# A hybrid decoder trunk with grouped experts: row numbers cast earlier, the first expert load by table held behind a row gather

## The reference

```python
scores = sigmoid(hf @ w_router)                      # 512 x 16 experts
group  = argmax(sum of the top 2 biased scores of each of 4 groups)
expert = the 2 best experts of that group            # 1024 assignments
gate   = their scores, normalised to sum 1
# tokens are sorted by expert into blocks; each block runs one expert:
yb  = (silu(xblk @ w_gate[e]) * (xblk @ w_up[e])) @ w_down[e]
out = zeros.at[buf_tok].add(yb * buf_w)              # back to the tokens
```

## Time and profile before

| | us |
|---|---|
| median of 3 runs | 1586.93 |
| lowest and highest | 1586.53 and 1590.78 |
| the profiled execution | 1591.75 |
| its span | 1590.0 |
| PE busy (88% of the span) | 1401.6 |
| DVE busy (41%) | 644.2 |
| ACT busy (20%) | 313.4 |
| POOL busy (5%) | 77.0 |

### The profile page before, as it was taken

One profiled execution on the slowest core, in us unless ns is written; L12 is line 12 of the kernel. 1 busy time (PEld: TensorE's weight loads), 2 busy tenths in 40 slices (PEclk: granted clock), 3 DMA queues, 4 the chain that ended last, 5 costly groups with the idle time before them and its releaser, 6 DMA issues.

```text
span 1590.0 us, 22845 instructions
## 1 busy us (share of the span) xinstructions
PE 1401.6 (88%) x9981; PEld 730.1 (46%) x9981; DVE 644.2 (41%) x1001; ACT 313.4 (20%) x525; POOL 77.0 (5%) x231
## 2 busy tenths in 40 slices
PE   5999999967888788889999958998998879999992
PEld 2445566536767633633333334555654353333331
DVE  1114334235756523723332334565742372233234
ACT  2221211133333202100000023442121310000002
POOL 7100000000000000000000020000000000000002
PEclk9999999987988989999999979999999898999997
DMA  9695676002000102899999962111100389999994
GB/s 359 218 316 185 212 243 205 3 29 92 3 2 3 56 0 119 338 392 425 350 426 421 398 217 88 54 54 53 53 1 1 136 349 391 427 347 426 422 382 172
DMA packets 87696, 332.63 MB, mean 209 GB/s; under 512 B 6456, under 2 KB 37420, under 8 KB 70188
## 3 DMA queue, kind: packets, MB, share of 16 engines
q1 hardware_dynamic: 74336, 290.04, 47.0%
q10 hardware_dynamic: 7788, 21.19, 3.4%
q0 software_dynamic: 5472, 19.93, 3.3%
HBM read 308.60 MB, written 22.54 MB: 208 GB/s over the span
## 4 chain that ended last, share of the span: by engine, by line
PE 70%; DVE 14%; DMA 9%; ACT 4%; issue 2%; POOL 0%; SPq 0%; DVEq 0%; ACTq 0%; POOLq 0%
PE banks L1352 16%; PE banks L1809 15%; PE banks L1830 9%; PE banks L1725 5%; DVE work L1945 5%; PE banks L1393 4%; PE banks L1341 4%; DMA h_features<-in_w_up_dram 3%; PE banks L1268 2%; DMA h_features<-in_w_down_dram 2%; PE banks L1709 2%; DVE work L1951 2%; DMA work<-h_rows,idx_tok 1%; PE banks L1518 1%; DMA ring<-in_w_ada_dram 1%
## 5 line engine op out<-in xcount | busy, mean ns | idle before, releaser
L1352 PE MATMUL banks<-h_features,ring 128*128 128x512 f32 (+1 forms) x656 | 293.0, 601 | 5.6 <-ACT h_features L936 4.0
L1809 PE MATMUL banks<-ring,work 128*64 128x512 f32 (+1 forms) x672 | 203.7, 603 | 3.7 <-issue 2.3
L1809 PE MATMUL banks<-work 128*64 128x512 f32 (+1 forms) x672 | 199.7, 595 | 0.0
L1352 PEld LDWEIGHTS banks<-h_features,ring 128*128 128x128 f32 (+1 forms) x656 | 122.0, 190 | 159.1 <-issue 155.6
L1945 DVE TENSOR_TENSOR work<-work,banks 128x256 f32<-128x256 f32 (+2 forms) x82 | 44.9, 569 | 180.0 <-PE banks L1809 132.3
L1809 PEld LDWEIGHTS banks<-ring,work 128*64 128x64 f32 (+1 forms) x672 | 60.6, 129 | 104.0 <-issue 99.3
L1945 DVE TENSOR_TENSOR work<-work 128x512 f32<-128x512 f32 (+9 forms) x212 | 102.4, 483 | 14.4 <-ACT work L1131 3.6
L1830 PE MATMUL banks<-ring,work 128*64 128x512 f32 (+1 forms) x288 | 98.7, 593 | 4.1 <-DMA h_features<-in_w_down_dram 3.5
L1809 PEld LDWEIGHTS banks<-work 128*64 128x64 f32 (+1 forms) x672 | 59.8, 130 | 68.8 <-issue 65.4
L1725 PE MATMUL banks<-y_features,ring 128*128 128x512 f32 x192 | 84.5, 602 | 6.4 <-DVE small L2474 6.4
L822 POOL DMA_INDIRECT work<-h_rows,idx_tok x20 | 19.0, 951 | 1286.4 <-DVE idx_tok L2610 963.8
(11 more groups left out here) (367 smaller groups left out, 1839.9 us busy)
## 6 DMA issues: line engine op xcount, KB each, us to landing
ring<-in_w_up_dram SPq DMA_DIRECT2D x16, 2048.0 KB, 14.7
work<-in_w_gate_dram SPq DMA_DIRECT2D x16, 2048.0 KB, 13.7
y_features<-in_w_ada_dram SPq DMA_DIRECT2D x28, 1024.0 KB, 6.0
work<-in_w_up_dram SPq DMA_DIRECT2D x14, 2048.0 KB, 14.1
ring<-in_w_down_dram SPq DMA_DIRECT2D x12, 2048.0 KB, 14.0
work<-in_w_down_dram SPq DMA_DIRECT2D x8, 2048.0 KB, 14.1
h_features<-in_w_down_dram SPq DMA_DIRECT2D x8, 2048.0 KB, 13.7
ring<-in_w_ada_dram SPq DMA_DIRECT2D x7, 2048.0 KB, 12.8
```

What stands on the lines that cost most here:

```text
L1352: ins = mm(PS[0:w, b, :], lhsT=W[:, k, c0:c0 + w], rhs=h[:, k, :], start=(k == 0), stop=(k == KD - 1))
L1809: ins = mm(PS[rows, bank, :], lhsT=xt[:, k, rows], rhs=w[:, k, :], start=(k == 0), stop=(k == KD - 1))
```

## The change

Two edits, both run once per layer.

- SP's first load by table waits, besides `table_ready`, until the gather of round 1's rows has landed (`gathered[l][1]`, the semaphore of the odd rows).
- The cast of `idx_tok` with its wait for `rank_ready` stands right behind the cast of the table, ahead of the pass count and of `idx_dest`.

```diff
@@ SP, the loads in the order of LOADS
                         if place not in expert_at:
                             if not expert_at:
                                 sp.wait_ge(sem("table_ready"), l + 1)
+                                sp.wait_ge(gathered[l][1], 16)
                             expert_at[place] = sp.value_load(table[0:1, place:place + 1], min_val=0, max_val=E - 1)
@@ DVE, choose(l)
                 link(dve.tensor_copy(table[:, 0:2 * E], tabf[:, 0:2 * E]))
+                dve.wait_ge(sem("rank_ready"), 2 * l + 2)
+                signal(dve.tensor_copy(idx_tok[:, 1:MAX_BLOCKS], PS[:, 6, 1:MAX_BLOCKS]), "rows_known")
                 link(tt(cmp16[:, 0, 0:7], ove[:, E - 1:E].to_broadcast([P, 7]), iota16[:, 0:14:2], ALU.is_gt))
                 link(dve.tensor_reduce(tabf[:, 32:33], cmp16[:, 0, 0:7], AX_X, ALU.add))
                 link(tsc(tabf[:, 32:33], tabf[:, 32:33], 1.0, ALU.add))
                 signal(dve.tensor_copy(table[:, 32 + l:33 + l], tabf[:, 32:33]), "table_ready")
                 link(stt(destf, selb, float(HALF_ROWS), selr, ALU.mult, ALU.add))
                 link(dve.tensor_copy(idx_dest[:, :], f2(destf)))
-                dve.wait_ge(sem("rank_ready"), 2 * l + 2)
-                signal(dve.tensor_copy(idx_tok[:, 1:MAX_BLOCKS], PS[:, 6, 1:MAX_BLOCKS]), "rows_known")
```

## The result

The changed kernel takes 1591.68 us (median of 22 runs) against 1586.57 us for the kernel before, timed beside it: 5.1 us more. The ratio is 1.0034, 95% interval 1.0017 to 1.0050, so slower, by 2.7 to 7.9 us. The forecast was 1592.9 us, in a range of 1588.5 to 1598.5. The ratio is an estimate of its own from all runs and can differ a little from the quotient of the two medians, here 1.0032; the same holds for the ratios further down.

A forecast was written before the change was run, and what follows sets the result against it. PE, busy nearly throughout the expert stages, was taken as the bound; round 1's gate, waiting for the second load, starts 3.0 us later per layer, so 1586.93 + 6.0 = 1592.9 us, range 1588.5 to 1598.5.

The forecast's parts named there:

- The views: Profile reading at round 1's gate: PE waits 4.7 us for the gather, but the second load landed only 0.7 us before use.
- rival D: Round 1 does not wait for the postponed loads; each layer gains 5.1 us, 1576.8 us; chance 0.06.
- The gather alone: Round 1's gather without weight loads beside it takes 4.2 us, so PE's 4.7 us wait at L1788 goes.
- A: Rival: the gather alone is quicker than 4.2 us, about 3.2; sum +3.4, 1590.3 us; chance 0.14.
- C: Rival: the gather takes 6.6 us, as the slow ones at the stage's end; +10.8, 1597.7 us; chance 0.13.
- Rival B: Slow clock shorter by 2 us, or third gather too late to matter; taken at +3.5, 1590.4 us; chance 0.12.
- The first load by table: SP's first gate load in layer 0 is issued at 670.70, 4.7 us later than 665.99, because of the added wait.
- The time of the two loads: First issue to second gate load's landing: 12.47 and 12.54 us without gathers, longer with the third gather; gate 3.0 us later.
- third gather: POOL's gather of round 3's rows starts earlier and shares bandwidth with the second gate load, moving its landing from 683.17 to 684.1.
- some 8 us: Sign: PE's longest wait would stand in front of round 1's gate at L1809, on DMA, some 8 us long.
- The clock: PE's slow stretch at 1.2 GHz behind the idle time stays 4.3 and 5.1 us; bounds -4.8 to +4.7 us in sum.
- Behind the gate: The stretch after round 1's gate only shifts, neither shorter nor longer; up loads stay hidden with 8 us to spare.

The follow-up runs named there:

- run with home 1: The change, plus round 1's gate matmuls taking weights from home 1 without waiting for homes 6 and 7 (output wrong): 1583.97 us, ratio to before 0.9983.
- third gather held: The change, plus POOL's gather of round 3's rows waiting until the second gate load by table landed: ratio to the kernel before 1.0027.
- cast with second gather held: Kernel before with the cast moved, no SP wait, POOL's gather of round 2's rows waiting for the second gate load's landing: 1583.86 us, ratio 0.9985.
- early table: Cast moved and round 2's gather held, plus SP's first load waiting only for the table's own cast: 1581.90 us, ratio to the kernel before 0.9981.
- only the second gather held: Kernel before with one edit, POOL's gather of round 2's rows waiting until the second gate load by table landed: ratio 0.9992.
- cast only: Kernel before with the idx_tok cast moved ahead and no added SP wait for the gather: ratio 1.0019.

## Why the prediction was right

*The views.* The decision lay in the 0.7 us by which the loads were ready before their use. This was read correctly from the landing of the load and the start of the gate: the chain of waits named only the gather, and who stopped there would have forecast a gain. The run with home 1 shows that nothing else keeps PE back at that point, and rival D falls with it.

*The gather alone.* Taken at 4.2 us with ends 2.2 and 6.6; it took 4.4 and 4.3. Rivals A and C fall with it. Rival B does too, with both of its conditions: the third gather did cost something, and the slow stretch was shorter by 0.5 and 0.9 us, not by 2. The Trainium skill's rule for a transfer from this queue in "DMA: Bandwidth & Descriptors", section "Anatomy of one DMA — SWDGE (gpsimd) path", gives 3.2 us, an estimate; here the trace has 4.4, and the measurement decides.

*The first load by table.* Forecast 4.7 us later; it was 4.9 and 4.7 us later within the entry stretch.

*The time of the two loads.* This term was too small. Forecast 13.4 and 13.5 us from the first issue to the landing of the second, measured 13.9 and 14.7. The base without gathers was nearly right: 12.47 and 12.54 forecast, 12.9 and 12.6 with the third gather held. The third gather was put at 0.9 us per layer; holding it back shortened this time by 1.0 and 2.1 us and moved the start by 0.9 and 1.7. Its first packets came 4.1 us after its start in both layers, close to the 4.5 of the forecast, so the overlap was placed rightly; why it cost twice as much in layer 1 stays open. So the start came 3.9 and 4.4 us later, not 3.0, and PE's wait was 10.2 and 10.5 us. The prediction names "some 8 us" for this wait where its own times, 674.9 to 684.1, give 9.2.

*The clock.* Taken as unchanged. The granted clock after (us, busy of PE, PEld, DVE, ACT, POOL, PEclk, DMA share, GB/s), in place of the earlier trace rows:

```profile
679.90:683.70 3.80, 3.80 (x20) 1.12 (x24) 0.00 (x0) 0.00 (x0) 0.00 (x0) 0.50 0.99 424
1317.70:1321.90 4.20, 4.20 (x20) 1.07 (x24) 0.00 (x0) 0.00 (x0) 0.00 (x0) 0.50 1.01 433
```

PE was at the 1.2 GHz level for 3.8 and 4.2 us after its idle stretch of 10 us, before for 4.3 and 5.1 after a shorter one. At half the clock that is 0.25 and 0.45 us back. Since the slow stretch was anything from 2.7 us (cast with second gather held, layer 1) to 5.7 us (early table, layer 0) long over all the kernels in which PE waited, without order by the idle time before it, this gain is chance.

*Behind the gate.* Forecast: shifted, nothing given back. In the trace 0.4 and 0.6 us came back over some 223 us, less than this part scatters between kernels. The prediction took a shorter stage behind as a sign against it; so small a difference can't serve as one. The up loads were hidden, as forecast.

*The sum.* Forecast +6.0 us; the trace has +7.6 in the entry stretches and -1.0 behind them, +6.6; the timed runs +5.1 (2.7 to 7.9). The load term was too small by 2.3 us in sum, and the two small gains happened to make up for 1.7 of it. So the way, the mechanism and the size of about 6 us are borne out; that the forecast came within 1 us of the median is luck in part.

*What I had missed,* though the sum stands without it: I valued the moved cast at the 1.0 us of its earlier start. The run with the cast alone shows that it suffices to end PE's wait for the gather. The wait on SP was thus not needed for what it removes, and it is the edit that costs: on top of the cast 3.1 us of entry stretch in layer 0 (32.26 against 29.15) and 3.7 in layer 1 (32.84 against 29.11), on top of the kernel before 4.1 and 6.2.

## What to carry to other kernels

When the chain of waits names a transfer, look up when the next operand of the same instruction landed; the gain ends there, and a wait that delays this operand can turn it into a loss. Where a small gather and large loads meet, don't hold the loads until the gather has landed. A gather that starts 0.8 to 0.9 us ahead of the load was enough to end the wait for it here, but that alone gained nothing (ratio 1.0019, interval 0.9996 to 1.0041), since the load then came last; the fastest kernel has the load first and both arriving together. Hold back what nobody needs soon (here the gathers of the rounds after), since it takes bandwidth from what is waited for: with the cast moved, the start came 1.9 and 1.6 us earlier by it.

## What the runs showed of the hardware

The time of the 0.5 MB gather depended on which transfer started first. It took 11.5 to 12.0 us in all cases seen where the first 2 MB load had been issued 0.3 to 0.6 us ahead of it (the kernel before, only the second gather held, early table), 4.9 to 8.1 us where it was 0.8 to 0.9 us ahead of the load (cast only and the two kernels built on it), and 4.1 to 4.7 us with no load until it had landed (the change and the three kernels built on it or with its wait). I had expected a share of the bandwidth and hence about the same time either way.

The packets of POOL's queue show two parts of it. The first ones came 1.6 to 1.8 us after the gather's start in the fourteen cases where no load had been issued ahead of it, and 4.1 to 4.5 us after it in the six where one had. And where the gather led by 0.8 to 0.9 us, it had moved 0.20 to 0.22 MB of its 0.52 when the load's first packets came in layer 0, and 0.36 to 0.43 MB in layer 1: there it took 7.4 to 8.1 us and 4.9 to 5.3. The load's first packets came 1.7 to 2.0 us after its issue in layer 0 and 2.4 to 2.7 us in layer 1, against 0.9 to 1.0 us where no gather had started just ahead. Why the packets of the later transfer start so late, and why the two layers differ in it, no run here settles.
